# S5 layer: projection and core as one stage of four chunks, a scan instruction, and input tables made during the FFN

## What is computed

```python
def s5_mixer(x, w_in, lam_re, lam_im, log_dt, b_re, b_im, c_re, c_im, d_skip, w_glu):
    u = (x @ w_in).astype(f32)                      # 512 x 1024
    lam = lax.complex(lam_re, lam_im); dt = jnp.exp(log_dt)[:, None]
    a_bar = jnp.exp(lam * dt)                       # 64 groups x 64 states
    b_bar = ((a_bar - 1.0) / lam)[..., None] * lax.complex(b_re, b_im)
    # h[t] = a_bar * h[t-1] + b_bar @ u[t], per group of 16 features
    # y[t] = real(c @ h[t]) + d_skip * u[t]
    hid = jax.nn.gelu(y, approximate=False)
    val, gate = jnp.split(hid @ w_glu, 2, axis=-1)
    return val * jax.nn.sigmoid(gate)
```

## Time and profile before

| | us |
|---|---|
| median of the runs | 2594.35 |
| the profiled execution's span | 2590.5 |
| TensorE busy in it | 2477.6 (96%) |
| VectorE busy | 1739.2 (67%) |
| ScalarE busy | 1051.9 (41%) |
| GpSimd busy | 589.9 (23%) |

### The profile page before, as it was taken

One profiled execution on the slowest core, in us unless ns is written; L12 is line 12 of the kernel. 1 busy time (PEld: TensorE's weight loads), 2 busy tenths in 40 slices (PEclk: granted clock), 3 DMA queues, 4 the chain that ended last, 5 costly groups with the idle time before them and its releaser, 6 DMA issues. The chain is left out here.

```text
span 2590.5 us, 41313 instructions
## 1 busy us (share of the span) xinstructions
PE 2477.6 (96%) x15961; PEld 2036.9 (79%) x15961; DVE 1739.2 (67%) x2869; ACT 1051.9 (41%) x1561; POOL 589.9 (23%) x447
## 2 busy tenths in 40 slices
PE   8998999999999989899999999998999999999998
PEld 6788887788887768899999999886776576767566
DVE  6945656467676784576666767676687567487667
ACT  4443233321212333355555555533344443344453
POOL 2404321430230020052333432440024001024001
PEclk9999999999999999999999999999999999999999
DMA  4321002346654252267776777853221211332121
GB/s 155 98 83 35 2 3 65 124 156 237 212 182 148 76 166 84 91 219 229 254 240 224 252 236 231 271 184 125 86 74 60 76 66 57 109 94 70 33 82 65
DMA packets 259968, 339.98 MB, mean 131 GB/s; under 512 B 24928, under 2 KB 217952, under 8 KB 259232
## 3 DMA queue, kind: packets, MB, share of 16 engines
q1 hardware_dynamic: 251840, 315.52, 37.6%
q0 software_dynamic: 4512, 15.99, 1.8%
q10 hardware_dynamic: 3456, 6.29, 0.8%
HBM read 318.63 MB, written 16.52 MB: 129 GB/s over the span
## 5 line engine op out<-in xcount | busy, mean ns | idle before, releaser
L3020 PE MATMUL ps<-x_feat_r,moe_w_hi 128*128 128x384 f32 x1408 | 405.1, 361 | 0.6 <-DVE x_feat_r L3132 0.6
L2545 DVE TENSOR_TENSOR moe_w_lo<-ring,moe_w_hi 128x2048 fp32r<-128x2048 f32 x144 | 316.1, 2196 | 126.8 <-ACT moe_w_hi L2540 126.6
L3023 PE MATMUL ps<-x_feat_r,moe_w_lo 128*128 128x192 f32 x1408 | 354.0, 251 | 0.0
L2540 ACT ACTIVATE moe_w_hi<-ring 128x2048 fp32r<-128x2048 f32 x144 | 254.8, 1770 | 93.5 <-PE ps L263 76.2
L3023 PEld LDWEIGHTS ps<-x_feat_r,moe_w_lo 128*128 128x128 f32 x1408 | 269.2, 191 | 0.3
L3020 PEld LDWEIGHTS ps<-x_feat_r,moe_w_hi 128*128 128x128 f32 x1408 | 264.3, 188 | 1.7 <-issue 1.4
L267 PE MATMUL ps<-x_free_r,ring_r 128*128 128x512 f32 x496 | 195.6, 394 | 0.0
L266 PE MATMUL ps<-ring_r,x_feat_r 128*128 128x256 f32 (+2 forms) x576 | 185.1, 321 | 0.0
L263 PE MATMUL ps<-x_feat_r,ffn_w_hi 128*128 128x512 f32 x352 | 139.3, 396 | 1.2 <-DVE ffn_w_lo L2488 1.2
L267 PE MATMUL ps<-x_feat_r,ffn_w_lo 128*128 128x512 f32 x352 | 139.4, 396 | 0.0
L266 PE MATMUL ps<-x_free_r,ffn_w_hi 128*128 128x512 f32 x352 | 138.5, 393 | 0.0
(11 more groups left out here) (661 smaller groups left out, 6407.1 us busy)
## 6 DMA issues: line engine op xcount, KB each, us to landing
ring<-in_moe_w SPq DMA_DIRECT2D x120, 1024.0 KB, 5.5
ring<-in_w_in SPq DMA_DIRECT2D x32, 1024.0 KB, 5.3
ring<-in_ffn_w SPq DMA_DIRECT2D x30, 1024.0 KB, 7.4
ring<-in_ada_t SPq DMA_DIRECT2D x48, 512.0 KB, 4.3
ring<-in_gdn_w_in SPq DMA_DIRECT2D x12, 1024.0 KB, 6.0
ring<-in_moe_w SPq DMA_DIRECT2D x24, 512.0 KB, 3.8
ring<-in_s_w_glu SPq DMA_DIRECT2D x8, 1024.0 KB, 5.6
ring<-in_w_out SPq DMA_DIRECT2D x8, 1024.0 KB, 6.2
```

The lines of the kernel that those rows point to most:

```text
L2540: self.prog.nc.scalar.activation(self.flat(self.hi, j % SPLITS, j), self.raw(j), ACT.Copy).then_inc(self.hi_done, 1)
L2545: self.prog.nc.vector.tensor_tensor(self.flat(self.lo, j % SPLITS, j), self.raw(j), self.flat(self.hi, j % SPLITS, j).bitcast(F32), ALU.su ...
L3020: mm = nc.tensor.matmul(out, wh[:, k, cs], both[:, k, :], start=(k == 0), stop=False)
L3023: mm = nc.tensor.matmul(out[:, 0:SLOTS], wl[:, k, cs], xg[0][:, k, :], start=False, stop=(k == KD - 1))
```

## The change

1. `Parameters` gets `input_powers`, called right after each `output_powers`. It makes an eighth of the input table in `x_tok`, and SyncE stores it to `p_dram`. C is loaded in eighths. The table of the pole's real and imaginary powers for one block (`a8`) becomes magnitude, cosine and sine (`pole`).
2. The five S5 stages become one, `s5_layer`, in four chunks b of eight pairs. The projection takes 8 tiles of 128 columns in the order 0, 4, 1, 5, ... so that two products feed one chunk. Input tables are loaded from DRAM by ScalarE's queue, turned by TensorE between the products, and copied by ScalarE.
3. The recurrence: the block input is rotated back by the pole's angle (`turn_in`), two `tensor_tensor_scan` instructions run over 512 elements with the magnitude as decay (`scan`), and the result is rotated forward (`turn_out`). The angles of 64 blocks are made first (`rotations`).
4. The lag table holds both groups of a pair in 32 columns (`wide`), the skip term is added to its diagonal by GpSimd (`add_skip`), and it is placed by 16 DMAs per chunk (`place`). `within` and the product with the states add up in one PSUM bank, so that `s5_outputs` and its additions are gone. Gelu reads the transposed result from PSUM.

```diff
@@ Parameters.loads (SyncE)
             sp.dma_start(self.prog.q_dram[:, :, n * self.QUADS:(n + 1) * self.QUADS], self.q
                          ).then_inc(self.q_stored, 16)
+            self.load_c(sp, n + 2)
+            sp.wait_ge(self.p_done, n + 1)
+            sp.dma_start(self.prog.p_dram[:, :, n * self.QUADS:(n + 1) * self.QUADS], self.p
+                         ).then_inc(self.p_stored, 16)
@@ Parameters.vector
             self.output_powers(dve, n)
+            self.input_powers(dve, n)
+    def input_powers(self, dve, n):
+        shape = [P, self.QUADS, STEP, GC]
...
+        tt(p_re, b_re, re, ALU.mult)
+        link(tt(tmp, b_im, im, ALU.mult))
+        link(tt(p_re, p_re, tmp, ALU.subtract))
+        tt(p_im, b_re, im, ALU.mult)
+        link(tt(tmp, b_im, re, ALU.mult))
+        tt(p_im, p_im, tmp, ALU.add).then_inc(self.p_done, 1)
@@ s5_layer, TensorE's order
+            keep_busy(prog, 7, 2)
+            project(0)
+            project(1)
+            project(2, 0)
+            inputs(0)
+            project(3)
+            project(4, 1, lambda half: table_bank_free(0, half))
+            inputs(1)
+            lags(0, lambda half: table_bank_free(1, half))
+            project(5)
+            project(6, 2, lag_bank_free)
+            inputs(2)
+            lags(1, lambda half: table_bank_free(2, half))
+            project(7, 3, lambda half: lag_bank_free(2 + half))
+            outputs(0)
+            turn_back(0, lambda half: table_bank_free(3, half))
+            inputs(3)
+            lags(2, lambda half: turn_bank_free(0, half))
+            outputs(1)
+            turn_back(1, lambda half: lag_bank_free(4 + half))
+            lags(3, lambda half: turn_bank_free(1, half))
+            outputs(2)
+            turn_back(2, lambda half: lag_bank_free(6 + half))
+            outputs(3)
+            pe.wait_ge(e_read, SC)
+            keep_busy(prog, E_BANK, 4)
+            turn_back(3, lambda half: turn_bank_free(2, half))
+            keep_busy(prog, E_BANK, 10)
@@ TensorE's waits in it
+            def inputs(b):
+                pe.wait_ge(t_copied, 4 * b + 4)
+                if b:
+                    pe.wait_ge(e_read, b)
+                pe.wait_ge(u_landed[b], 2 * 16 * STEP)
...
+            def outputs(b):
+                pe.wait_ge(placed[b], 32 * STEP)
+                if b:
+                    pe.wait_ge(y_copied, 2 * b)
...
+                pe.wait_ge(h_ready, b + 1)
@@ VectorE
+            for n in range(3):
+                proj.split_lo(dve, n)
+            skip_diagonals()
+            rotations()
+            proj.split_lo(dve, 3)
+            proj.split_lo(dve, 4)
+            turn_in(0)
+            proj.split_lo(dve, 5)
+            scan(0)
+            turn_out(0)
...
+                for r in range(2):
+                    m = nc.vector.tensor_tensor_scan(t[:, r].rearrange("p q j -> p (q j)"), decay,
+                                                     h[:, r].rearrange("p q j -> p (q j)"), 0.0, ALU.mult, ALU.add)
@@ SyncE
+            def place(b):
+                sp.wait_ge(zeroed, b + 1)
+                sp.wait_ge(skip_added, 2 * b + 2)
+                for i in range(STEP):
+                    n, at = (STEP - i) * GC, (STEP - 1 - i) * GC
+                    for gp in range(2):
+                        rows = LR * b + GC * gp
+                        sp.dma_start(mix[b][at:at + GC, :, gp, i * GC:], lag[rows:rows + GC, :, 0:n]).then_inc(placed[b], 16)
+            for n in range(RING):
+                next_tile(RING + n)
+                turn_u(n)
+            turn_u(4)
+            place(0)
+            turn_u(5)
+            turn_u(6)
+            place(1)
+            turn_u(7)
+            place(2)
+            place(3)
+            for b in range(SC):
+                sp.wait_ge(y_ready, 2 * b + 2)
+                W.load(sp, W.issued)
+                W.issued += 1
@@ GpSimd
+            widen(0)
+            widen(1)
+            pool.wait_ge(skip_ready, 1)
+            for b in range(SC):
+                zero(b)
+                add_skip(2 * b)
+                add_skip(2 * b + 1)
+                if b + 2 < SC:
+                    widen(b + 2)
@@ DVE in dense_parts, before the last additions
                 dve.wait_ge(beside.q_stored, 16 * beside.n_q)
+                dve.wait_ge(beside.p_stored, 16 * beside.n_q)
```

More of the change, by code:

```diff
@@ L1708 @@
 PI_IN = 3.1415925
-GSTEP = 8
+SC = 4
+SQ = PAIRS // SC
+QUAD = SQ // 2
+IN_ORDER = [gp * SC + b for b in range(SC) for gp in range(2)]
+LR = 2 * GC
 def reduce_angle(nc, link, x, tmp, shift=0.0):
@@ L2014, in s5_tables @@
[L2014 to L2028 removed]
+        at = (STEP - 1 - i) * GC
@@ new lines, in turn_bank_free, with turn_tables @@
+            def turn_bank_free(b, half):
+                pe.wait_ge(gelu_done, 4 * b + 3 + half)
+            def turn_tables(b, r, free):
+                if r == 0:
+                    pe.wait_ge(p_landed, 16 * (b + 1))
+                for half in range(2):
+                    if free:
+                        free(half)
+                    for j in range(QUAD):
+                        m = nc.tensor.transpose(ps[:, MISC_BANK + half, j * P:(j + 1) * P], into[:, r, half * QUAD + j, :], ident)
+                    m.then_inc(turned, 1)
@@ new lines, in _ @@
+            rotations()
[5 more added lines that the diff above has]
+            turn_out(0)
+            proj.split_lo(dve, 6)
+            turn_in(1)
+            proj.split_lo(dve, 7)
+            scan(1)
+            turn_out(1)
+            turn_in(2)
+            scan(2)
+            turn_out(2)
+            split_hid(0)
+            turn_in(3)
+            scan(3)
+            turn_out(3)
@@ L2315, in _ @@
+            for b in range(1, SC):
+                split_hid(b)
         @st.gpsimd
@@ new lines, in widen, with zero @@
+            def widen(b):
+                if b >= 2:
+                    pool.wait_ge(lag_ready, 2 * (b - 2) + 2)
+                for gp in range(2):
+                    rows = TOKENS[gp]
+                    for r in range(2):
+                        link(nc.gpsimd.tensor_copy(room.wide[b % 2][rows, r, :, gp * GC:(gp + 1) * GC], s5.bbar[rows, r, chunk(b), :]))
+                pool.sem_inc(wide_ready, 1)
+            def zero(b):
+                pool.wait_ge(proj.product, SC + b + 1)
+                nc.gpsimd.memset(mix[b], 0.0).then_inc(zeroed, 1)
+                pool.wait_ge(zeroed, b + 1)
@@ new lines, in add_skip @@
+            def add_skip(s):
+                pool.wait_ge(lag_copied, s + 1)
+                rows, qs = lag_rows(s // 2), half_pairs(s)
+                nc.gpsimd.tensor_tensor(lag[rows, qs, 0:GC], lag[rows, qs, 0:GC], skip[rows, qs, :], ALU.add
+                                        ).then_inc(skip_added, 1)
+                pool.wait_ge(skip_added, s + 1)
+            for i in range(2):
+                m = nc.gpsimd.memset(room.wide[i], 0.0)
+            link(m)
+            widen(0)
+            widen(1)
```

733 lines of the change are left out of this document (330 added, 403 removed).

## The result

The changed kernel takes 2612.21 us (median of four runs, 2610.43 to 2614.26) beside 2594.74 us for the kernel before, a ratio of 1.007 with a 95% interval of 1.0055 to 1.0084: 17.5 us slower. The forecast was 2592, its range ended at 2606. The profiled execution's span is 2609.8 us (2590.5 before).

The account below looks back on a forecast made before the run. TensorE was taken to bound the FFN, no engine the whole S5 layer. FFN +8.0 us and S5 stage -10.0 us gave -2.0 on 2594.35, rounded 2592 us; range 2580 to 2606.

Parts of the forecast that it names:

- The stall: First FFN run: `input_powers` of n=1 and n=2 delay tile 15's split, so TensorE stalls 5.9 us near 615.
- cold start: FFN, behind the stall: TensorE is cold and loses 2.1 us, making +8.0 us together.
- the hidden six of the eight calls: FFN: all `input_powers` calls except n=1 and n=2 of the first run cost nothing.
- The stage's walk: New S5 stage along TensorE's list: ends at 968.7, -12.3 us; -10.0 with 2.3 us for cold starts.
- Waits for u: S5 stage: TensorE's four waits for turned u ahead of inputs(0) to inputs(3), 8.1 us in all.
- The low clock: S5 stage: cold starts behind waits of 2.6 us or longer, up to 2.1 each, 2.3 us allowed in all.
- place(3): S5 stage's last chunk: TensorE waits 4.4 us for the lag placement; 16 DMAs at 0.51 us, 8.2 us a place.
- Rival D: S5 stage: SyncE becomes the bound, a DMA costs the same whatever its pieces; 2602 at 0.8 us each; chance 0.17.
- A scan: VectorE in the S5 stage: 0.69 us each; up to 4 us the walk's end doesn't move.
- rival E: S5 stage: a scan costs over 4 us and the stage follows VectorE; 2598 at 6 us, 2606 at 8; chance 0.06.
- B: Rival: the FFN hides `input_powers`, costing 0 instead of 8 us; 2584; chance 0.20.
- C: Rival: the S5 stage is shorter, lag products at 0.119 us and fewer cold starts; 2586 to 2588; chance 0.15.

Follow-up runs that it names:

- e5: As e1, with the store of the second eighth of the input table queued one tile earlier on SyncE: 2602.0 us, ratio 1.0039.
- e1: Changed kernel with the `input_powers` of n=1 and n=2 in the first FFN run moved behind later lo splits, their stores following: 2610.0 us, ratio 1.0058.
- e4: Changed kernel with two output table loads later on ScalarE's queue, load_q(1) behind next_tables(1), load_q(2) behind copy_lags(0): 2609.5 us, ratio 1.0058.
- e2: Changed kernel with turned loads reading complete `p_dram` without waiting for u, all ahead of the first place (result not valid): 2598.4 us, ratio 1.0015.
- e7: Changed kernel with each place cut in two, SyncE issuing the eight DMAs of the first groups, GpSimd's queue the second: 2600.3 us, ratio 1.0035.
- e6: Changed kernel with S5 work reordered: lags ahead of inputs (chunks 1, 2) and of turn_back, chunk 3's tables turned late in project(7): 2597.3 us, ratio 1.0022.
- e3: Changed kernel with six keep_busy products ahead of each of the four waits for u: 2608.0 us, ratio 1.0044.
- e11: Changed kernel with eight keep_busy products in the wait for place(3): 2612.1 us, one run.
- e10: Changed kernel with each place DMA carrying only four of its eight pairs, 64 pieces instead of 128: 2608.4 us, one run.
- e9: Changed kernel with every pair of scans issued twice, eight more scans on VectorE: 2610.5 us, one run.
- e8: e4, e5, e6 and e7 together on the changed kernel: 2577.6 us, ratio 0.9940 to the kernel before.

## Why the prediction was wrong, step by step

**The FFN: right in mechanism and place, 2 us short.** The stall was forecast at 5.9 and measured at 6.0. Up to the next tiles 9.0 are lost, of which 0.4 was lost ahead of it and 2.6 is the cold start (2.1 forecast); one more comes in at the end of the FFN, no more than executions differ there. e5 shows that the hidden six of the eight calls cost nothing, as forecast, and e1 that the store counts as much as the call.

**The stage's walk: the order of the waits right, their sizes wrong.** Against the walk, from the timeline of the changed kernel:

- *Waits for u*, 18.4 for 8.1: **+10.3** (3.2, 2.5, 2.0 and 2.6). This is the step that failed most. The walk gave u 9.8 us from the end of a product to the landing (its terms add up to 9.5); it took 12.6 in chunk 0 and 11.7 in chunk 1 (product 3 ends at 884.1, inputs(1) starts at 895.83). I had taken the landings from the earlier trace rows, where the turned loads had only the stores of u beside them, and didn't count the tables on ScalarE's queue as traffic. e4 shows this for the first wait. For the second, e2 shows that it stays though u is ready, and e4 that it stays with the table moved beside its store. For the third, e7 shows SyncE's place. The fourth is a table load again by the rows of the changed kernel and of e6; no run moved it.
- *The low clock*, 2.3 us in all forecast, "they are short". Short ones weren't free: behind the 2.09 us for Gelu the lag products took 5.32 for 3.68. Four times `inputs` 14.1 for 7.6 us, **+6.5**, of which 5.8 is clock (2.08 at full speed); project(3) 6.5 for 5.4, +1.0; lags 17.1 for 14.0, +3.1, of which 2.4 is clock and the rest the price (3.68 full, 3.5 forecast); outputs 23.9 for 22.0, +1.9, of which 1.5 is clock. Of these 12.5 us some 10.7 are clock. e3 and e11 show that the clock is the cause of the durations; e3 also shows that only a part of this comes back when the clock alone is mended.
- *place(3)*, 5.9 for 4.4: **+1.5**. The places took 0.65 to 0.72 us per DMA (gaps included) where I took 0.51. My step from pieces to time was wrong in kind: I scaled by pieces between two rows, and e10 shows that the pieces don't matter at this size. The 0.79 of that row isn't the price of an issue either, whose median there is 0.618; why that row is longer wasn't looked into. Rival D had the right mechanism (a DMA costs the same whatever its pieces) and its walk 972.6 to 975.8 for such a price, though only one of the four places was above the 11 us that were its sign; it had only the issue time, not what the delay of u does to the clock.
- *Tables*, 1.9 for 1.2: +0.7.

The sum is 25.0, less the 2.3 allowed for cold starts 22.7; measured is 157.6 - 136.2 = 21.4. Redone, the walk's own sums hold within 0.4 us a step.

**VectorE: right where it counts.** The rotations took 16.8 us for 16.4; GpSimd's copies had ended at 851.5, ahead of them, as the prediction had it; the copies at 904.69 lie beside scan(1), whose two scans took 2.51 for 2.33. A scan was mis-sized, 1.22 for 0.69 (9.5 for all eight), at no cost, and e9 excludes rival E. E's 6 and 8 us are 2.9 and 3.9 times its dearest row, not "two to three times". B had no part in it, since the stall came, nor had C: the lag products took 0.23 each at full clock.

**Behind the stage: not in the sum.** `s5_glu` began in the kernel before at the low clock, behind a wait of 3.2; in the changed kernel fourteen keep_busy products and a wait of 1.7 stand ahead of it. 20 us from 2.7 ahead of its first product, before and after:

```profile
980.00:1000.00 20.00, 17.31 (x122) 0.83 0.25 76
```

```profile
1001.40:1021.40 20.00, 18.32 (x149) 1.00 0.35 113
```

The first 28 products start 0.21 us apart before and 0.12 after, which makes 2.6 us. That is where the 2.1 us come back; it wasn't tried alone.

**The range** was too narrow for one reason: each wait's error was taken as independent and small, but each wait drew the same three things after it (later u, low clock, later place). D's bound of 2606 priced one of them.

## What to carry to other kernels

When a walk through a new order rests on a DMA's way, price the way with the traffic that the change itself adds, on whichever queue, and price each wait of some 4 us as itself plus 1.5 to 2 us of slow products behind it. Where an engine waits for data that another engine makes, look first for work of its own that needs none of it: the new order of e6, with the lag products ahead of the waits, was worth 13 us, keeping the clock up in the waits no more than 3. A row of many merged DMAs can hide a pause: ask for each group by its own window before dividing by the count. Count DMAs, not bytes, for the engine that issues them, and look at what else stands in its list.

## What the runs showed of the hardware

- A DMA of this kind (SBUF to SBUF, 64 or 128 short pieces) costs SyncE 0.60 us to issue whatever its pieces, a turned load from DRAM 0.46 (3.68 for eight; 4.77 beside a table load), GpSimd's queue 0.52 for the same place DMA. Why the first two differ wasn't tried.
- One table of 1152 KB under way lifts the median landing of 32 KB loads from 2.2 to 4.8 us (e4 and the changed kernel), that of the loads issued right beside it from 1.9 to 5.5.
- After a pause of 4 to 6 us the granted clock is at its lower level, 1.2 GHz of 2.4: the same 64 products take 3.68 instead of 2.08 us. After one of 1.9 us a part of them is slow (2.92, e3). Short pauses differ: behind 1.21 us in e7 the 32 products of outputs(3) took 3.63, behind 1.00 in e8 1.97.
- A scan of 512 elements takes 1.22 us.
